# A third set of sparse tokens in the expert layer, an even spread of row products, and layer norms in two passes

## What is computed

```python
v1, i1 = lax.top_k(s1, PEER_TOPK); v2, i2 = lax.top_k(s2, PEER_TOPK)
...
experts = jnp.take_along_axis(cand_idx, pos, axis=-1)   # 8 heads x 16 of 16384 experts per token
gates = jax.nn.softmax(vals, axis=-1)
u = expert_u[ec]
a = jnp.einsum('cd,chkd->chk', xc, u)
w = jax.nn.gelu(a) * gc
out = jnp.einsum('chk,chkd->cd', w, expert_v[ec])

def layer_norm(x, g, b):
    mu = jnp.mean(xf, -1); var = jnp.mean(jnp.square(xf - mu), -1)
    return (xf - mu) * lax.rsqrt(var + LN_EPS) * g + b
```

## Time and profile before

| | us |
|---|---|
| median of three executions | 1772.64 |
| the profiled execution | 1773.28 |
| its span in the trace | 1771.5 |
| TensorE busy in the span | 1735.8 |
| expert layer by blocks and rows in the trace | about 440 to 1022 |

### The profile page before, as it was taken

The page is one execution under the profiler, slowest core; times in us unless marked ns, Lnnn a source line. Parts: engine busy times, 40 slices in busy tenths (PEclk is TensorE's granted clock), DMA queues, the critical chain, the costliest instruction groups (busy, mean ns, idle before and its releaser), DMA issues.

```text
span 1771.5 us, 29553 instructions
## 1 busy us (share of the span) xinstructions
PE 1735.8 (98%) x11793; PEld 1482.8 (84%) x11793; DVE 1119.2 (63%) x2415; ACT 240.8 (14%) x599; POOL 301.4 (17%) x282
## 2 busy tenths in 40 slices
PE   8999999999999899999999999999999999999996
PEld 7898576986999899999999868699955978699942
DVE  4752432898657888799533533279974763379964
ACT  1014520110414111000000011111100001011100
POOL 0010000145433444444422200000000000000000
PEclk9999999999999999999999999999999999999998
DMA  7534234499999999999999844365554435354551
GB/s 276 190 122 164 72 119 143 155 337 372 414 416 416 405 407 398 373 412 415 415 417 418 344 202 160 126 223 172 171 173 166 167 121 191 117 170 167 170 182 50
DMA packets 76609, 439.62 MB, mean 248 GB/s; under 512 B 8566, under 2 KB 8656, under 8 KB 37840
## 3 DMA queue, kind: packets, MB, share of 16 engines
q1 hardware_dynamic: 42624, 305.15, 46.4%
q0 software_dynamic: 32592, 125.92, 18.3%
q10 hardware_dynamic: 1280, 6.95, 1.0%
HBM read 432.67 MB, written 5.24 MB: 247 GB/s over the span
## 4 chain that ended last, share of the span: by engine, by line
PE 81%; DMA 9%; DVE 8%; issue 1%; ACT 1%; POOL 0%; SPq 0%; POOLq 0%; DVEq 0%
PE ps L1139 16%; PE ps L921 14%; PE ps L540 10%; DMA arena<-u_rows,sparse_pairs 7%; PE ps L584 7%; PE ps L913 7%; PE ps L1177 4%; PE ps L623 3%; PE ps L498 3%; DVE arena L1912 2%; PE ps L776 2%; PE ps L823 2%; PE ps L789 1%; PE ps L934 1%; PE ps L1008 1%
## 5 line engine op out<-in xcount | busy, mean ns | idle before, releaser
L913 PE MATMUL ps<-xT,ring 128*128 128x150 f32 x2048 | 268.4, 293 | 0.0
L921 PE MATMUL ps<-arena,ring 128*128 128x150 f32 (+1 forms) x2048 | 266.3, 292 | 0.8 <-DMA ring<-stream 0.8
L913 PEld LDWEIGHTS ps<-xT,ring 128*128 128x128 f32 x2048 | 264.4, 191 | 0.1
L921 PEld LDWEIGHTS ps<-arena,ring 128*128 128x128 f32 x2048 | 262.3, 190 | 1.5 <-issue 1.5
L540 PE MATMUL ps<-ring,arena 128*128 128x512 f32 x416 | 181.4, 592 | 0.4 <-ACT arena L1487 0.4
L2033 DVE SCALAR_TENSOR_TENSOR arena<-arena,sparse_dots 128x1024 f32<-128x1024 f32 x105 | 134.7, 1283 | 73.4 <-DMA arena<-v_rows,sparse_pairs 68.2
L2501 POOL DMA_INDIRECT arena<-v_rows,sparse_pairs x107 | 132.8, 1241 | 224.9 <-DVE arena L2033 180.4
L1912 DVE CUSTOM_DVE_ANT_0 arena<-arena 128x1024 f32<-128x1024 f32 x107 | 127.9, 1223 | 66.9 <-DMA arena<-u_rows,sparse_pairs 66.3
L2501 POOL DMA_INDIRECT arena<-u_rows,sparse_pairs x107 | 132.4, 1238 | 167.9 <-DVE sparse_dots L1912 143.7
L2464 POOL TENSOR_SCALAR stat<-stat 128x1 f32<-128x1 f32 (+2 forms) x23 | 4.4, 190 | 913.8 <-DVE stat L2205 705.7
L540 PEld LDWEIGHTS ps<-ring,arena 128*128 128x128 f32 x416 | 78.0, 190 | 93.0 <-issue 92.3
(11 more groups left out here) (341 smaller groups left out, 2244.2 us busy)
## 6 DMA issues: line engine op xcount, KB each, us to landing
ring<-stream SPq DMA_DIRECT2D x288, 1024.0 KB, 7.5
arena<-second_params POOLq DMA_DIRECT2D x6, 1024.0 KB, 5.2
arena<-kv_scratch POOLq DMA_DIRECT2D x2, 2048.0 KB, 14.2
kv_scratch<-arena ACTq DMA_DIRECT2D x2, 1024.0 KB, 10.7
arena<-held_params ACTq DMA_DIRECT2D x1, 2048.0 KB, 16.5
arena<-u_rows,sparse_pairs POOLq DMA_INDIRECT x107, 13.7
arena<-v_rows,sparse_pairs POOLq DMA_INDIRECT x107, 11.2
arena<-second_params POOLq DMA_DIRECT2D x1, 1536.0 KB, 6.5
```

What stands on the lines that cost most here:

```text
L913: ins = pe.matmul(ps[:, o % 2, 0:DENSE], w[:, (o % 2) * D + k * P:(o % 2) * D + (k + 1) * P], xT[:, k, 0:DENSE], start=(k == 0), stop=(k = ...
L921: ins = pe.matmul(ps[:, 4 + k // 2, c:c + DENSE], w[:, (o % 2) * D + k * P:(o % 2) * D + (k + 1) * P], H[:, n, :], start=False, stop=last, ...
```

## The change

The diff does four things. Two tokens move from the dense to the sparse side as a third set, C, each on 64 partitions, so that two fetches of `u` and two of `v` cover it; `DENSE` becomes 148. Its x (laid out by a VectorE copy into `x_wide_c`, turned by 8 products on TensorE before the up pass, copied by ScalarE) and its sums lie in the two tiles of `xres`. GpSimd issues four more small loads for its pair lists, and the fold gets 8 more products. The row products of the first half start from `DOTS_FIRST` = 70 and go to 114, not from 74 to 116. `LAST_ADDS` becomes 13, so that 205 of 218 turns stand ahead of the residual of the first tile. And each layer norm subtracts the mean and multiplies by g before it waits for the inverse root, then multiplies by that and adds b: two operations for three.

```diff
-SPARSE = SPARSE_A + SPARSE_B
+SPARSE_C = 2
+SETS_C = P // SPARSE_C
+SPARSE = SPARSE_A + SPARSE_B + SPARSE_C
...
-CHUNKS = PAIRS_HALF + PAIRS_B
+PAIRS_C = P // SETS_C
+SET_AT = (0, PAIRS_HALF, PAIRS_HALF + PAIRS_B)
+CHUNKS = PAIRS_HALF + PAIRS_B + PAIRS_C
+PAIR_LOADS = 3 + SETS_B + 2 * SPARSE_C
...
-DOTS_TURN = 74
-TURNS_UP = 116
+TURNS_UP = 114
...
-LAST_ADDS = 14
+LAST_ADDS = 13
...
+        x_wide_c = sparse_sum[:, 0, :].rearrange("p (k t e) -> p k t e", k=KT, t=SPARSE_C)
+        x_of_set = (x_sparse[:, 0, :], x_sparse[:, 1, :], xres[:, 0, :])
+        sum_of_set = (sparse_sum[:, 0, :], sparse_sum[:, 1, :], xres[:, 1, :])
...
-            pe.wait_ge(xres_T_ready, 2)
+            pe.wait_ge(x_wide_c_ready, 1)
+            pe.wait_ge(xres_T_ready, 4)
+            for k in range(KT):
+                ins = pe.matmul(ps[:, 2 + k // 4, (k % 4) * P:(k % 4 + 1) * P],
+                                x_wide_c[:, k].rearrange("p t e -> p (t e)"), ident, start=True, stop=True)
+            ins.then_inc(x_c_psum, 1)
...
-                for part, (name, n) in enumerate((("fold", SPARSE_A), ("fold_b", SPARSE_B))):
-                    c = (k % 2) * T + (T - SPARSE_A, DENSE)[part]
+                for part, (name, n) in enumerate((("fold", SPARSE_A), ("fold_b", SPARSE_B), ("fold_c", SPARSE_C))):
+                    c = (k % 2) * T + (T - SPARSE_A, DENSE + SPARSE_C, DENSE)[part]
...
+            act.wait_ge(x_c_psum, 1)
+            for q in range(2):
+                ins = act.copy(xres[:, 0, q * 512:(q + 1) * 512], ps[:, 2 + q, :])
+            ins.then_inc(x_c_ready, 1)
...
+            dve.wait_ge(xT_by_dve, 8)
+            dve.tensor_copy(x_wide_c, xT[:, :, DENSE:DENSE + SPARSE_C].unsqueeze(3)
+                            .to_broadcast([P, KT, SPARSE_C, SETS_C])).then_inc(x_wide_c_ready, 1)
             best16(range(4, 16), sc[:, 0], top_v, ti, DOTS_SCORES)
...
-                    a, b = ((DOTS_TURN, TURNS_UP), (TURNS_UP, TURNS_DOWN))[hf]
+                    a, b = ((DOTS_FIRST, TURNS_UP), (TURNS_UP, TURNS_DOWN))[hf]
                     row_turns(a + (b - a) * (g + 1) // GROUPS)
...
+                    dve.wait_ge(moments_ready, 2 * n + i + 3)
+                    parts = (slice(0, 512), slice(512, D)) if n == 5 else (slice(0, D),)
+                    for c in parts:
+                        v = xres[:, i, c]
+                        ins = dve.scalar_tensor_tensor(v, v, stat[:, 50 + 2 * i:51 + 2 * i], ln_p[:, n, 0, c],
+                                                       ALU.subtract, ALU.mult)
+                    link(ins)
                     dve.wait_ge(ln_rstd, 2 * n + 3 + i)
-                    for c in ((slice(0, 512), slice(512, D)) if n == 5 else (slice(0, D),)):
+                    for c in parts:
                         v = xres[:, i, c]
-                        link(dve.tensor_scalar(v, v, stat[:, 50 + 2 * i:51 + 2 * i], stat[:, 54 + i:55 + i],
-                                               ALU.subtract, ALU.mult))
-                        link(dve.tensor_tensor(v, v, ln_p[:, n, 0, c], ALU.mult))
-                        dve.tensor_tensor(v, v, ln_p[:, n, 1, c], ALU.add).then_inc(x_ready, 1)
+                        dve.scalar_tensor_tensor(v, v, stat[:, 54 + i:55 + i], ln_p[:, n, 1, c],
+                                                 ALU.mult, ALU.add).then_inc(x_ready, 1)
...
+                    for t in range(SPARSE_C):
+                        for n in range(2):
+                            pool.dma_start(pairs[SETS_C * t:SETS_C * (t + 1), n, PAIRS_HALF + PAIRS_B:],
+                                           pairs_out_b[c_first + t:c_first + t + 1, n, 0:P]
+                                           .rearrange("o (e c) -> o e c", c=PAIRS_C)).then_inc(pairs_in, 16)
```

35 lines of the change are left out of this document (21 added, 14 removed).

## The result

The changed kernel takes 1778.02 us (median of 11 executions, 1775.98 to 1780.44) against 1773.47 us for the kernel before beside it: a ratio of 1.0027, with a 95% interval of 1.0019 to 1.0035. It is slower by 0.27%. The profiled execution took 1778.02 us and has a span of 1776.2 us, 4.7 more than before.

A forecast was written before the change was run, and what follows sets the result against it. TensorE was taken to bound the kernel up to 996.5 us, the DMA-fed row supply close behind. Residual -2.1, clock +2.4, fold +1.8, norms -1.1 and -1.9 sum to -0.9 us: 1771.7 us, no change; 8-in-10 range 1762 to 1777.5.

The forecast's parts named there:

- one of its own signs of being wrong: The prediction called itself wrong if VectorE waits for TensorE before the residual, or if the residual starts after 997.
- What bounds the kernel: Up to 996.5 us TensorE sets the end, with the row supply, set by the DMA engines, close behind.
- TensorE stays the bound: Down pass: rows keep up, the full 11.95 us come with no clock loss; 1759.5 us, chance 0.2.
- its stall stays: Second group of gates: the even spread doesn't remove TensorE's wait for one-hots; 1766.4 us, chance 0.05.
- The sum on TensorE: Expert stage: 6.85 us from fewer columns plus 7.0 from the stall, less 1.9 for set C's x: 11.95 us earlier.
- I take it that all of the unused time is used: DMA engines, 584 to 996.5 us: all of at most 10.0 us unused is regained for row fetches.
- the slower rival: Row add 205 ahead of the residual: unused DMA time stays unused; half regained gives 1776.7 us, none 1781.7; chance 0.15.
- none of the 10 us, all of it: Bounds on how much of the DMA engines' unused time before the residual is regained; the forecast took all.
- The ring's refill: After the down pass the weight stream loads ahead, 2.11 MB still to come, competing with the last rows before the residual.
- The clock loss: TensorE's products behind the residual run at a lower clock after some 10 us idle: 2.4 us lost, bounds 0 and 7.4.
- the fold's growth: The fold grows from 32 to 48 passes, +1.8 us.
- The norms: Layer norms in two operations: -1.1 us for three waits of TensorE, -1.9 us for the last norm.

## Why the prediction was wrong

The forecast was 1771.7 us, no change; it came out 0.27% slower, and one of its own signs of being wrong was there: the residual started after 997.

**What bounds the kernel** was right: after the change VectorE waits for rows and no longer for TensorE, and the place is row add 205. That TensorE stays the bound, or that its stall stays, is ruled out by 13.50 us of waiting and by 143.00 busy of 143.

**The sum on TensorE** was right in its terms. The stall went, and alone the even spread measured 7.1 us (6.3 by the medians) against 7.0. The down pass ended 10 us earlier, not 11.95, as this execution reached the up pass late, at 442.09 us. In the run with work ahead of the residual, whose code is the same up to there, the up pass began at 440.47 and the down pass ended at 984.67, where the forecast had 984.55.

**The step that failed** is "I take it that all of the unused time is used". Of the 10.0 us that the DMA engines had left unused, some 7 came back from 584 to 861 (411, 409 and 415 GB/s in place of 402, 292 and 414), and 2.9 stayed unused there, 1.4 of them from 704 to 727, at 391 GB/s. Why, no run shows. In the forecast's own sum, 2.9 us less put the residual at some 997.4; the run with work ahead of the residual, with the same three rates, had it at 997.6. In the change's own trace 2 us more were lost ahead of 584 (0.8 MB less than before, most of it from 340 to 360). That loss is this execution's: in the run with work ahead of the residual, whose code is the same up to there, it is missing. The windows are of the kernel before, the change and that run:

```profile
340.00:360.00 20.00, 20.00 (x100) 17.75 (x100) 13.67 (x68) 2.59 (x6) 7.80 (x8) 1.00 0.68 247
340.00:360.00 20.00, 20.00 (x100) 17.77 (x99) 13.63 (x67) 4.07 (x8) 7.79 (x8) 1.00 0.59 216
340.00:360.00 20.00, 20.00 (x100) 17.79 (x99) 13.71 (x67) 2.46 (x5) 7.79 (x8) 1.00 0.68 254
```

So the net was 5 of the 10 us, the half, and the residual started at 999.41 and not 994.5; the slower rival had 999.5. That this rival fits so closely is in part luck, as that execution's own loss is in it. I gave that rival a chance of 0.15, and of the bounds "none of the 10 us, all of it" I took one end; the middle gave 1776.7 on a median of 1772.64, 0.23% slower, which is nearly what was measured. The ring's refill was sized right: 2.24 MB from 985 to 999, 2.11 expected.

**After the residual.** The clock loss was 1.8 us against 2.4, the fold's growth 2.1 against 1.8. Missing was the dip behind the fold, 1.3 us, which the 2-column products bring: with 64 columns it is gone (8.68 us for the products in the change, 7.36 in both kernels with the wide fold and no wait ahead of it).

**The norms:** -3.3 us in the traces and -3.7 alone, against -3.0. Right in the sum; the five inner norms gave 1.7, not 1.1.

**What the sum could not show** is that it added parts of opposite sign. The spread and the norms alone give -9.4 us. Set C takes 13.8 from that: it makes TensorE's work 5 us shorter in a stage whose DMA engines are full, and gives them four row sets more, 2.1 MB or 5 us at 417 GB/s. The residual can be moved ahead (200 turns) or the rows made quicker, but TensorE then meets the last row add ahead of the fold, and pays in clock.

## What to carry to other kernels

Where TensorE and the DMA engines are both full in a stage, work moved from one to the other counts twice, as here: 5 us less on one side and 5 us more on the other. So read, at the place where they meet, who waits and for how long, and move no more than half of that. (The half follows from this count; no run tried a smaller set C.) Measure the parts of a change one by one, as a part that gains can hide one that loses. And before a transfer's rate is taken as the engines' limit, shift its buffers by some tens of bytes: 32 unused bytes gained 0.26% here (0.16 to 0.36).

## What the runs showed of the hardware

**The start address of the row buffers.** Row fetches of 4 KB into buffers that start at a multiple of 256 bytes ran at 423 to 425 GB/s together with the weight stream, from 861 to 985, at every other start here (32, 64, 128, 224 past one) at 417 to 418. The forecast had taken 417 as what the engines can do. The Trainium skill, on the page DMA: Bandwidth & Descriptors, section How a descriptor splits into AXI transactions, has a rule for it: a transaction must start at a multiple of 256 bytes, so the first one of a descriptor that doesn't start there begins at the multiple below, and the bytes ahead of the start are fetched for nothing. The trace agrees as to the 256, where 64 and 128 changed nothing. By that rule the loss would also grow with the bytes in front of the start, and would strike the stream's ring at 128 past, too; here 32 and 224 past cost the same, and the ring's shift gave 425 GB/s in place of 424, too little to tell.

**The clock and narrow work.** A fold of 32 passes of 64 and 42 columns ran at 3.5 us, and the 64 products behind it at 7.39. With 16 passes of 2 columns among them the products behind the fold took 8.7 to 10.1 us in each of the seven kernels in which that fold had begun at full clock, though TensorE was busy throughout: the granted clock went to 0.50 at the fold's end or right behind it. With those 16 widened to 64 columns and no wait ahead, they took 7.36, at a clock of 1.00, in both kernels tried.

**A wait ahead of narrow work costs more than one ahead of wide work.** In eight traces TensorE waited 2.77 to 13.50 us ahead of the 64 products of 128 columns behind the residual, and these took 8.7 to 10.1 us in place of 7.38: 1.4 to 2.7 us lost, and no more after the longest wait (9.18) than after 2.77 (9.01). After 3.76, 5.77 and 7.66 us of waiting ahead of the fold, the fold alone lost 4.6 to 5.0 us (10.3 us in place of 5.6, or of 5.3 where set C's part is 64 columns wide), as the clock stood at 0.50 from its first pass until it was over. And after a wait of 1.79 us it fell within the fold, as this window of TensorE shows (its clock is the third figure from the end):

```profile
1012.30:1017.00 4.70, 4.70 (x24) 4.70 (x24) 1.25 (x3) 0.00 (x0) 0.00 (x0) 0.50 0.00 0
```
